# Two transformer blocks in one launch: how the second block's stages hand over to each other, and which engine copies and multiplies attention's probabilities

## The chip, the cores and the metric

One core of a Trainium2 chip runs the whole program. The metric is the device time of one launch in microseconds (us). Times are lower-is-better. The engines are TensorE (PE; PEld is its weight load), VectorE (DVE), ScalarE (ACT), GpSimd (POOL) and SyncE (SP), which issues most transfers.

## What is computed

The input is one sequence of 1024 tokens of width 1024, all in fp32. `first_block` has two layers: a projection, three token mixers (sliding-window attention, retention, gated linear attention), an output projection and a normed residual. `second_block`, which the change is about, has two layers of this form, cut to what matters:

```python
for l in range(DEPTH):                                   # DEPTH = 2
    hc = rmsnorm(h_ctx, g_pre_mix[l]) * (1.0 + csc1) + csh1      # 256 context rows
    hx = rmsnorm(x, g_pre_mix[l]) * (1.0 + sc1) + sh1            # 1024 rows
    q, k, v, u, gv, f = jnp.split(hx @ w_in[l], ...)             # and the same of hc (k, v alone in the last layer)
    attn = latent_window_attention(rope(q), rope(k), v, ck, cv, sink[l])   # band of 3 blocks of 128, plus 256 context keys, plus a sink
    sgu = spatial_gating(gelu(u), gelu(gv), w_sgu[l], b_sgu[l], g_sgu[l])
    four = fourier_mix(f)                                        # real part of a DFT over tokens and 64-wide groups
    y = merge_heads(attn, sgu, four, g_mix[l], w_out[l])         # three rmsnorms, then @ w_out
    x = x + g1 * rmsnorm(y, g_post_mix[l])
    hx2 = rmsnorm(x, g_pre_ff[l]) * (1.0 + sc2) + sh2
    x = x + g2 * rmsnorm(jnp.square(relu(hx2 @ w1)) @ w2, g_post_ff[l])    # D_FF = 4096; the same for h_ctx in layer 0
```

The softmax of attention is `exp(s - max) / (sum + exp(sink - max))`, and the probabilities that are multiplied by the values are already divided.

## The kernel before

**Products in three terms.** Activations lie transposed: a partition is one of 128 features, the columns are tokens, 512 at a time (two halves, b = 0 and 1) or the 256 of the context (b = NB). A weight matrix comes in chunks of 128 outputs x 1024 inputs, 512 KB each. To keep fp32 accuracy in the faster fp32r format, each operand is split into a rounded part and a rest. SyncE loads a chunk into `wraw` (L1690), ScalarE rounds it into `whi` (`split_high`, L1750), and GpSimd computes the rest `wlo` (`split_low`, L1736). The activations have `h_hi` (ScalarE, `high`, L1799) and `h_lo` (VectorE, `low`, L2120 on). TensorE then does 16 high products (h_hi and h_lo with whi, L2453) and 8 low products (h_hi with wlo, L2460) into one of two banks of `lin`. `wraw`, `whi`, `wlo` and the banks have two slots each, taken in turn by even and odd chunks. Semaphores count what is done: `w_hi`, `w_split`, `lin_done` (a chunk's last low product), `lin_free` (its bank evacuated). ScalarE's order of work in a chunk is: wait for `lin_done`, evacuate the bank, then round the weights of the chunk after next into the slot that this chunk has left. So `lin_done` also guards `whi`, and through it `wlo`.

**Stages of the second block.** Layer 0: projection of half 0 (`project`, 12 chunks), of the context, of half 1; the Fourier transform (`fourier`, 16 steps); the merges of half 0, half 1 and the context (`merge`, 8 chunks each); the feed-forwards of half 0, context, half 1 (`feed_forward`, 4 groups of 8 chunks of hidden units and 8 of outputs). Layer 1: the context's keys and values (2 chunks), both halves, the transform, two merges, two feed-forwards. Two of a projection's chunks are done token-major (`token_half`, L2562 on, products of L2574). Each engine has its own program, written out in the same order; they meet only through semaphores.

**Norms.** A norm's squares come from ScalarE (`square`, L1755) one feature block after another, VectorE adds them up (`add_square`, L2106), TensorE sums over partitions with a matrix of ones (L2430) and ScalarE makes the reciprocal root with a logarithm and an exponential (`root_pre`, `root_post`, `mix_roots`). VectorE scales the activations (`scale`, L2116), and `high` and `low` split them (L1804 or L1806; L2125 or L2127). The squares and scales of the next stage's norm are put beside a stage's chunks by hand; `high` and `low` of all 8 blocks come at the start of the next stage, after this stage's last chunk has read `h_hi` and `h_lo`. The first two chunks of a stage are multiplied as a pair (`high_pair`, L2464), each block as it becomes ready.

**Attention** is cut into steps of 4 heads and 128 queries, 40 in layer 0 and 32 in layer 1. Step i goes beside the i-th chunk or transform step, from the projection of half 1 on. TensorE's scores (L2533 to L2538); VectorE's maximum (`maximum`, L2148); ScalarE's exponentials (L1821); VectorE's reciprocal and its multiplication of the probabilities (`normalize`, L2175 and L2177); TensorE's transposes (`turn`, L2497), key and value head 0 and then 1, one chunk later; two copies out of `bankT` for each, by VectorE (L2166) and ScalarE (L1831); and the products with the values (L2559) at the head of the step after. On VectorE the additions of squares and the scales come before the copies (`attend`, L2180).

**The first block** uses the same chunks and slots in its own loop (L486 to L830, L1113 to L1163, L1395 to L1412).

## Time and profile before

| | |
|---|---|
| median of 3 runs | 4272.48 us (4271.44 to 4273.14) |
| the profiled execution | 4272.9 us, of which 4270.7 us from its first to its last instruction |
| mean granted TensorE clock | 0.956 of full speed |
| TensorE busy | 89% |
| VectorE, ScalarE, GpSimd busy | 51%, 40%, 36% |
| read from HBM | 397 MB, 95 GB/s over the span |

The first block ends at about 1313 us of the span, the second runs from there to the end. Busy shares are means over stages that differ. What counts is what TensorE waits for and where, and at which clock it runs afterwards. In the rows, a time in square brackets is how long the engine was idle just before the instruction, and behind the arrow stands what ended that idle time. Instructions of PE are grouped in a timeline only if they follow each other with the same operands.

### The profile page before, as it was taken

What the parts mean: (1) busy time and instruction counts of PE and PEld (TensorE: products, weight loads), DVE (VectorE), ACT (ScalarE), POOL (GpSimd) and SP (SyncE); (2) the same over time, 40 slices, a digit from 0 to 9 for tenths busy, and PEclk for the clock granted to TensorE, in tenths of its full rate; (3) what the DMA queues carried; (4) which work ended last, traced back from release to release, by engine and by line L of the source; (5) the groups of instructions that cost most, each with busy time, mean ns of one, the idle gap of its engine ahead of it and who ended that gap; (6) DMA issues with size and microseconds to landing.
All of it is one profiled execution on the core that took longest, in us unless ns stands there. A gap on an engine that the chain in (4) does not pass through costs nothing. (4 is left out here: it accounts for less than half of the span.)

```text
span 4270.7 us, 60415 instructions
## 1 busy us (share of the span) xinstructions
PE 3805.2 (89%) x22828; PEld 3059.4 (72%) x22828; DVE 2166.8 (51%) x2741; ACT 1714.6 (40%) x2935; POOL 1555.4 (36%) x704
## 2 busy tenths in 40 slices
PE   4989999999996798877999788999799779999997
PEld 3867767667665677656788777887677668877886
DVE  5435536445444566657325647325666664347225
ACT  3345345354353444444223334224444453234222
POOL 1433434334332322223444564443322224444443
PEclk8999999999998899988999999999899999999999
DMA  6423424333323221112232443332321122332223
GB/s 236 138 98 123 136 104 143 116 114 124 131 94 103 84 70 50 50 50 78 90 94 93 127 138 100 94 93 85 89 69 50 50 69 86 95 95 89 93 93 108
DMA packets 127195, 421.17 MB, mean 99 GB/s; under 512 B 17408, under 2 KB 19088, under 8 KB 126352
## 3 DMA queue, kind: packets, MB, share of 16 engines
q1 hardware_dynamic: 120080, 407.45, 29.6%
q10 hardware_dynamic: 6912, 10.90, 0.7%
q8 instruction: 141, 2.31, 0.2%
q14 instruction: 62, 0.51, 0.0%
HBM read 397.32 MB, written 6.29 MB: 95 GB/s over the span
## 5 line engine op out<-in xcount | busy, mean ns | idle before, releaser
L1739 POOL TENSOR_TENSOR wlo<-wraw,whi 128x1024 fp32r<-128x1024 f32 x454 | 1097.5, 2423 | 1859.4 <-ACT whi L1753 1858.9
L2453 PE MATMUL lin<-h_hi,whi 128*128 128x512 f32 (+1 forms) x2016 | 764.6, 386 | 107.1 <-DVE h_lo L2127 39.3
L2453 PE MATMUL lin<-h_lo,whi 128*128 128x512 f32 (+1 forms) x2016 | 749.0, 379 | 0.0
L1753 ACT ACTIVATE whi<-wraw 128x1024 fp32r<-128x1024 f32 x454 | 477.3, 1055 | 651.4 <-PE lin L2460 555.5
L2453 PEld LDWEIGHTS lin<-h_hi,whi 128*128 128x128 f32 x2016 | 398.0, 197 | 194.7 <-issue 112.5
L501 POOL TENSOR_TENSOR wlo<-wraw,whi 128x1024 fp32r<-128x1024 f32 x130 | 314.3, 2418 | 586.9 <-ACT whi L596 586.9
L2453 PE MATMUL lin<-a_hi,whi 128*128 128x512 f32 (+1 forms) x1280 | 479.4, 381 | 46.7 <-ACT whi L1753 38.8
L2453 PE MATMUL lin<-a_lo,whi 128*128 128x512 f32 (+1 forms) x1280 | 474.9, 377 | 0.0
L2460 PE MATMUL lin<-h_hi,wlo 128*128 128x512 f32 (+1 forms) x2016 | 461.5, 372 | 4.9 <-POOL wlo L1739 4.9
L2453 PEld LDWEIGHTS lin<-h_lo,whi 128*128 128x128 f32 x2016 | 397.5, 197 | 68.7 <-issue 3.3
L2460 PEld LDWEIGHTS lin<-h_hi,wlo 128*128 128x128 f32 x2016 | 352.0, 189 | 71.5 <-POOL wlo L1739 8.8
L2341 DVE TENSOR_TENSOR a_lo<-tmp,a_hi 128x512 fp32r<-128x512 f32 (+3 forms) x160 | 311.9, 1949 | 116.8 <-ACT a_hi L2025 114.3
L1122 PE MATMUL lin<-h_hi,whi 128*128 128x512 f32 x832 | 343.3, 413 | 8.2 <-DVE h_lo L846 8.2
L1122 PE MATMUL lin<-h_lo,whi 128*128 128x512 f32 x832 | 332.0, 399 | 0.0
L2453 PEld LDWEIGHTS lin<-a_hi,whi 128*128 128x128 f32 x1280 | 247.0, 193 | 104.1 <-issue 46.3
L2460 PE MATMUL lin<-a_hi,wlo 128*128 128x512 f32 (+1 forms) x1280 | 295.9, 375 | 2.4 <-POOL wlo L1739 2.2
L2453 PEld LDWEIGHTS lin<-a_lo,whi 128*128 128x128 f32 x1280 | 247.0, 193 | 46.6 <-issue 0.5
L2366 DVE TENSOR_TENSOR y<-lin,y 128x512 f32 (+3 forms) x120 | 76.5, 637 | 397.0 <-PE lin L2460 396.9
L2021 ACT ACTIVATE tmp<-lin 128x512 f32<-128x512 f32 (+1 forms) x160 | 88.4, 553 | 451.8 <-PE lin L2460 421.7
L2460 PEld LDWEIGHTS lin<-a_hi,wlo 128*128 128x128 f32 x1280 | 225.1, 188 | 52.5 <-POOL wlo L1739 4.6
L2106 DVE TENSOR_TENSOR tmp<-tmp 128x512 f32<-128x512 f32 (+1 forms) x165 | 166.3, 1008 | 176.9 <-ACT tmp L1763 172.1
L2338 DVE TENSOR_TENSOR tmp<-tmp 128x512 f32<-128x512 f32 (+1 forms) x160 | 132.1, 826 | 236.6 <-ACT tmp L2021 229.6
(339 smaller groups left out, 5998.7 us busy)
## 6 DMA issues: line engine op xcount, KB each, us to landing
wraw<-in_w SPq DMA_DIRECT2D x544, 512.0 KB, 3.5
mod_ring<-in_w_ada SPq DMA_DIRECT2D x96, 512.0 KB, 4.6
mod_ring<-in_w_mod SPq DMA_DIRECT2D x32, 512.0 KB, 4.6
wraw<-in_dft_tokens SPq DMA_DIRECT2D x32, 512.0 KB, 3.5
turn<-turn SPq DMA_DIRECT2D x144, 64.0 KB, 2.1
first_ring<-in_w_mod SPq DMA_DIRECT2D x16, 512.0 KB, 17.1
tmp<-tmp SPq DMA_DIRECT2D x80, 64.0 KB, 2.0
x<-in_x ACTq DMA_DIRECT2D x2, 2048.0 KB, 21.1
```

The costliest lines, as they stand in the source:

```text
L501: nc.gpsimd.tensor_tensor(wlo[:, s, :], wraw[:, s, :], whi[:, s, :].bitcast(F32), ALU.subtract)\
L1122: nc.tensor.matmul(bank[c % 2], whi[:, c % 2, k * P:(k + 1) * P], h[:, k, :], start=(k == 0 and h is h_hi), stop=False)
L1739: nc.gpsimd.tensor_tensor(wlo[:, s, 0:D], wraw[:, s, 0:D], whi[:, s, 0:D].bitcast(F32), ALU.subtract)\
L1753: nc.scalar.activation(whi[:, s, 0:D], wraw[:, s, 0:D], ACT.Copy).then_inc(*w_hi.one)
L2021: nc.scalar.activation(tmp[:, 4 + s, 0:w], bank[s][:, 0:w], ACT.Relu).then_inc(*lin_free.one)
L2106: nc.vector.tensor_tensor(total, total, tmp[:, slot, 0:w], ALU.add).then_inc(*sig["add"].one)
L2338: nc.vector.tensor_tensor(tmp[:, 2 + s, 0:w], tmp[:, 4 + s, 0:w], tmp[:, 4 + s, 0:w], ALU.mult).then_inc(*a_sq.one)
L2341: nc.vector.tensor_tensor(a_lo[:, unit, 0:w].rearrange("p o n -> p (o n)"), tmp[:, 2 + s, 0:w], a_hi[:, unit, 0:w].rearrange("p o n -> p ( ...
L2366: nc.vector.tensor_tensor(part, bank[s][:, 0:p.w], part, ALU.add).then_inc(*lin_free.one)
L2453: nc.tensor.matmul(bank[s][:, 0:p.w], whi[:, s, k * P:(k + 1) * P], h[:, k, 0:p.w], start=(k == 0 and h is parts[0]), stop=False)
L2460: last = nc.tensor.matmul(bank[s][:, 0:p.w], wlo[:, s, k * P:(k + 1) * P], parts[0][:, k, 0:p.w], start=False, stop=(k == KB - 1))
```

## The change

It has nine parts; the diff below is cut to the core of each.

1. *A semaphore for the high products.* `hi_used` counts chunks whose high products are done. `split_high` waits for it and no longer comes behind the evacuation: ScalarE rounds the weights of the chunk after next before it waits for `lin_done` (`refill`, and `split_high` at the head of `hidden` and in `outputs`). `split_low` gets a wait of its own for `lin_done`. The first block gets the same.

```diff
             def split_low(g, s):
                 pool.wait_ge(*w_hi.after(g, 1))
+                pool.wait_ge(*lin_done.after(g, -1))
...
             def split_high(g, s):
+                act.wait_ge(*hi_used.after(g, -1))
                 act.wait_ge(*chunk_in[s].after(g, 0))
...
             def hidden(gi, grp, j, s, w):
+                split_high(gi + 2, s)
                 act.wait_ge(*lin_done.after(gi, 1))
                 act.wait_ge(*a_ready.after(grp, j - 1))
                 nc.scalar.activation(tmp[:, 4 + s, 0:w], bank[s][:, 0:w], ACT.Relu).then_inc(*lin_free.one)
-                split_high(gi + 2, s)
```

2. *Chunks by blocks.* The last chunk of a projection, transform or merge, and the first of a projection or merge, are multiplied block by block, all three terms of a block together. After each block of a last chunk `h_used` is raised, and the next stage's `high` of that block waits for it. Both weight parts must be there before the first block.

```diff
+            def by_blocks(g, s, p, when=None, end=None):
+                pe.wait_ge(*lin_free.after(g, 1))
+                pe.wait_ge(*w_hi.after(g, 1))
+                pe.wait_ge(*w_split.after(g, 1))
+                for k in range(KB):
+                    if when:
+                        pe.wait_ge(*when(k))
+                    for n, (w, h) in enumerate(((whi, h_hi), (whi, h_lo), (wlo, h_hi))):
+                        last = nc.tensor.matmul(bank[s][:, 0:p.w], w[:, s, k * P:(k + 1) * P], h[:, k, 0:p.w],
+                                                start=(k == n == 0), stop=(k == KB - 1 and n == 2))
+                        if k == KB - 1 and n:
+                            last.then_inc(*(hi_used if n == 1 else lin_done).one)
+                    if end is not None and k < KB - 1:
+                        last.then_inc(*h_used.one)
...
-            def high(kind, n, k):
+            def high(kind, n, k, end=None, last=None):
                 act.wait_ge(*sig["scaled"].after(n.no, k + 1))
+                if end is not None:
+                    act.wait_ge(*(h_used.after(end, k + 1) if k < KB - 1 else lin_done.after(last, 1)))
```

3. *`high` and `low` of the next stage beside the last chunk.* On ScalarE, in the projection (the merge is alike, the transform does it in its last two steps); on VectorE all 8 `low` follow the last chunk's other work, in the merge ahead of the last square of the post-norm:

```diff
+                    if s == last:
+                        if nxt:
+                            for k in range(KB - 1):
+                                high("pre", nxt, k, end_of(l, "in", p.b), p.in_at + s)
+                        refill(p.in_at + s, s)
+                        if nxt:
+                            high("pre", nxt, KB - 1, end_of(l, "in", p.b), p.in_at + s)
...
             def merge(l, b):                      # VectorE
-                    if k == 0:
-                        for j in range(KB):
-                            low("mix", n, j)
...
+                    if k == KB - 1:
+                        for j in range(KB):
+                            low(kind, following, j)
                     add_square("post", post, k, POST_SUMS)
```

TensorE's sum for that post-norm stays at the head of the next merge.

4. *Norms earlier.* In the first projection the squares for the context rows come beside chunks 2 to 5 and those for half 1 beside chunks 5 to 8 (`sums_beside`, with two blocks of `y` as room for the latter); the context's projection makes none and scales half 1 at chunks 3 to 6. The merge's squares for the next merge come at chunks 1, 2 and 4 and its roots at 5 (before: 2 to 5, and 6); the transform's squares at steps 9 and 10 and its roots at 11 (before: 9 to 11, and 12), the scales at 12 to 14.

```diff
+        def sums_beside(l, b):
+            if b == 0:
+                return [(pre_mix(l, NB), 2, bankO), (pre_mix(l, 1), 5, bankT)] if l == 0 else [(pre_mix(l, 1), 5, bankO)]
+            return []
```

5. *Sums behind products.* TensorE's sum over partitions for a projection's norm and for the first feed-forward's norm comes after the chunk's high products instead of before them. In the feed-forward the sum for the last stage's post-norm comes after 4 chunks instead of 1, its root at chunk 3, and the updates of the residual come two a chunk at chunks 4 to 7 instead of one a chunk at 1 to 7.

6. *The probabilities' multiplication on ScalarE.*

```diff
+            def normalize(l, i):                  # ScalarE
+                r, n = i % 2, sum(blocks_of(step_of(l, i)[0])) * P
+                act.wait_ge(*rden_ready.after(STEP_AT[l] + i, 1))
+                for kv in range(2):
+                    nc.scalar.activation(probs[r][:, kv, 0:n], probs[r][:, kv, 0:n], ACT.Copy, scale=rden[:, r, kv:kv + 1])\
+                      .then_inc(*pn_ready.one)
...
-            def normalize(l, i):                  # VectorE
+            def denominators(l, i):
                 link(nc.vector.tensor_tensor(esum[:, r, :], esum[:, r, :], esink[:, r, :], ALU.add))
-                link(nc.vector.reciprocal(rden[:, r, :], esum[:, r, :]))
-                for kv in range(2):
-                    nc.vector.tensor_scalar(probs[r][:, kv, 0:n], probs[r][:, kv, 0:n], rden[:, r, kv:kv + 1], None, ALU.mult)\
-                      .then_inc(*pn_ready.one)
+                nc.vector.reciprocal(rden[:, r, :], esum[:, r, :]).then_inc(*rden_ready.one)
```

ScalarE's order in a step is: exponentials, the next weights (in the projection and the merge), the copy for head 0, the multiplications, then squares, weights (in the transform), evacuation, the copy for head 1.

7. *VectorE's copies first.* Its copy for head 0 and the reciprocal come before the additions of squares.

8. *Values turned into another bank.* The transposes of the values go to `bankO` instead of the chunk's own bank, so that bank is free once it is copied.

9. *The transform's last two steps by blocks* (`last_blocks`), with all three terms of a block together; the third sum of the mix norm goes to `bankO` where that is free.

## Rows read from the trace of the kernel before

**Rows 1.** Page, busy us of each engine, share of the span and instructions

```profile
PE 3805.2 (89%) x22828; PEld 3059.4 (72%) x22828; DVE 2166.8 (51%) x2741; ACT 1714.6 (40%) x2935; POOL 1555.4 (36%) x704
```

**Rows 2.** Busy by window: length, PE, PEld, DVE, ACT, POOL busy (count), clock, DMA, GB/s

```profile
1399.00:1463.00 64.00, 46.14 (x311) 42.79 (x310) 23.36 (x29) 33.20 (x54) 28.24 (x12) 0.84 0.32 99
1978.00:2350.00 372.00, 358.36 (x1542) 291.05 (x1542) 163.16 (x152) 120.89 (x168) 155.79 (x65) 0.99 0.29 92
```

**Rows 3.** Waits of TensorE by releaser: us in total, times, longest

```profile
PE lin L2453 <- ACT whi L1753: 71.2, 55, 5.8
...
PE lin L1144 <- ACT whi L596: 3.6, 4, 0.9
```

**Rows 4.** Timeline of TensorE at handovers: start, us, operation, [idle before]

```profile
1471.36 0.77 PE L2453 MATMUL lin<-h_hi,whi 128*128 128x512 f32 x1 [6.87 <-DVE h_lo L2127]
...
1765.90 0.76 PE L2453 MATMUL lin<-h_hi,whi 128*128 128x512 f32 x1 [3.00 <-DVE h_lo L2125]
...
3000.81 0.77 PE L2453 MATMUL lin<-h_hi,whi 128*128 128x512 f32 x1 [6.53 <-DVE h_lo L2127]
...
3016.60 2.54 PE L2574 MATMUL lin<-whi,h_hi 128*128 128x256 f32 x16 [2.44 <-ACT whi L1753]
...
3096.33 0.77 PE L2453 MATMUL lin<-h_hi,whi 128*128 128x512 f32 x1 [5.14 <-DVE h_lo L2127]
...
3450.17 1.10 PE L2430 MATMUL bankT<-tmp,ones 128*128 128x512 f32 x2 [2.65 <-DVE tmp L2106]
...
3519.83 0.73 PE L2453 MATMUL lin<-h_hi,whi 128*128 128x512 f32 x1 [5.19 <-DVE h_lo L2127]
```

**Rows 5.** Timeline of TensorE at sums over partitions of the next norm

```profile
1377.16 1.22 PE L2430 MATMUL bankO<-tmp,ones 128*128 128x256 f32 x2 [6.59 <-DVE tmp L2106]
...
1449.31 2.08 PE L2430 MATMUL bankO<-tmp,ones 128*128 128x512 f32 x2 [6.97 <-DVE tmp L2106]
...
3495.15 2.07 PE L2430 MATMUL bankT<-tmp,ones 128*128 128x512 f32 x2 [6.70 <-DVE tmp L2106]
```

**Rows 6.** Timeline of ScalarE and TensorE, from hidden units to outputs of a feed-forward

```profile
2032.69 0.60 ACT L2021 ACTIVATE tmp<-lin 128x512 f32<-128x512 f32 x1 [3.38 <-PE lin L2460]
2033.18 1.05 ACT L1753 ACTIVATE whi<-wraw 128x1024 fp32r<-128x1024 f32 x1
...
2124.49 0.47 PE L2453 MATMUL lin<-a_hi,whi 128*128 128x512 f32 x1 [1.37 <-ACT whi L1753]
```

**Rows 7.** Timeline of VectorE before the attending projection of layer 1

```profile
3086.01 9.51 DVE L2116 SCALAR_TENSOR_TENSOR staged<-x,cols,tmp 128x512 f32<-128x512 f32 x8
3095.44 5.38 DVE L2127 SCALAR_TENSOR_TENSOR h_lo<-staged,cols,h_hi 128x512 fp32r<-128x512 f32 x8
```

**Rows 8.** Timeline of GpSimd in the context's feed-forward

```profile
2419.26 4.75 POOL L1739 TENSOR_TENSOR wlo<-wraw,whi 128x1024 fp32r<-128x1024 f32 x2 [2.47 <-ACT whi L1753]
2426.49 4.95 POOL L1739 TENSOR_TENSOR wlo<-wraw,whi 128x1024 fp32r<-128x1024 f32 x2 [2.47 <-ACT whi L1753]
```

**Rows 9.** Attention: groups by form (busy, mean ns), then timeline rows of ScalarE and TensorE

```profile
L2177 DVE TENSOR_SCALAR staged<-staged,rden 128x640 f32<-128x640 f32 x128 | 72.4, 608 | 2.2
...
L1804 ACT ACTIVATE h_hi<-q 128x512 fp32r<-128x512 f32 x16 | 8.8, 626 | 1.7 <-DVE q L2116 1.7
...
1659.66 2.00 ACT L1753 ACTIVATE whi<-wraw 128x1024 fp32r<-128x1024 f32 x2 [0.90 <-PE lin L2677]
...
1693.79 1.30 PE L2497 MATMUL bankT<-ident,staged 128*128 128x128 f32 x5 [3.10 <-DVE staged L2166]
```

**Rows 10.** The chain that ended last, in order of time: start, us, line, count

```profile
3519.83 9.11 PE lin L2453 x32
3533.46 3.63 PE lin L2453 x16
3538.91 3.63 PE lin L2453 x16
...
3567.83 7.25 PE lin L2453 x30
```

More of the change, by code:

```diff
@@ L1677, in merge_point, with merge_squares, mix_bank, scales_at @@
             return MERGE_POINT + MERGE_ROWS[l].index(b) * KB + k
+        def merge_squares(k):
+            return {1: MIX_SQUARES[0:2], 2: MIX_SQUARES[2:4], 4: MIX_SQUARES[4:8]}.get(k, ())
+        def mix_bank(n, part):
+            if part < 2:
+                return turnT[part]
+            return turnT[0] if n.rows.l == 0 and n.rows.b == 1 else bankO
+        def scales_at(first, s):
+            return range(4 * (s - first - 5), 4 * (s - first - 4)) if 5 <= s - first < 7 else ()
         @block.sync
@@ L1902, in project @@
             def project(l, p):
-                n, nxt, attending = pre_mix(l, p.b), next_in(l, p.b), p.b == 1
-                if p.in_no and not (l and p.context):
-                    for k in range(KB):
-                        high("pre", n, k)
-                for s in range(2 if l and p.context else IN2):
+                nxt, attending, last = next_in(l, p.b), p.b == 1, 1 if l and p.context else IN2 - 1
+                for s in range(last + 1):
                     if l and p.b == 0 and s == 0:
@@ L1988, in merge @@
             def merge(l, b):
[L1989 removed]
+                p, post, g = Rows(l, b), post_mix(l, b), merge_at(l, b)
                 prev, nxt = before_merge(l, b), next_merge(l, b)
                 ff = pre_ff(l, FF_ROWS[l][0]) if nxt is None else None
[L1992 to L1993 removed]
+                kind, following = ("mix", nxt) if nxt else ("pre", ff)
                 if prev:
@@ L2599, in project @@
                 n, nxt, g, attending = pre_mix(l, p.b), next_in(l, p.b), p.in_at, p.b == 1
+                last = 1 if l and p.context else IN2 - 1
                 def ready(k):
                     return norms["pre"]["ready"].after(n.no, k + 1)
-                for s in range(2 if l and p.context else IN2):
+                for s in range(last + 1):
                     also = None
@@ L2626, in project @@
                         token_half(g + GV2, p, s - GV2, True)
-                    else:
+                    elif s and not ends:
                         low_products(g + s, s % 2, p, h_parts)
```

474 lines of the change are left out of this document (270 added, 204 removed).

## The prediction

> **What bounds the kernel now.** I read the page's busy line first. TensorE is busy for 3805.2 of 4270.7 us, no other engine for more than half [rows 1]. So the end is set by TensorE's work, its waits, and what a wait does to its clock. The busy time by stage shows where it waits: the projection of the 256 context columns keeps TensorE busy for 46.14 of 64 us at a granted clock of 0.84, while a feed-forward of 512 columns has 358.36 of 372 us at 0.99 [rows 2]. A granted clock of 0.84 is a mix of TensorE's two levels, 1.2 and 2.4 GHz, and in this trace the low level follows a wait. The list of waits says for whom: the largest sum, 71.2 us, is for ScalarE's rounded weights [rows 3]. The timeline of TensorE then shows four kinds of places.
>
> First, handovers, where a stage's last chunk is done and the next stage's activations still have to be rounded (ScalarE) and their rest taken (VectorE). Eleven of the eighteen stages begin after a handover that the diff touches; six such places stand in [rows 4]. Second, sums over partitions before which VectorE's additions are late [rows 5]. Third, the change from hidden units to outputs in the feed-forward [rows 6]. Fourth, attention's steps, with waits of a few us where the squares for the next norm are put between its copies [rows 9].
>
> Units: a chunk of 512 columns takes TensorE 5.45 us (two starts in the chain) at full clock, of which 3.63 us are its high products; the first pair of chunks takes 7.25 us for 30 matmuls in steady work and 9.11 us for 32 after a handover, 1.4 us more than 32 in proportion [rows 10]. So a wait of 5 us costs about 6.5.
>
> **The sum.** It is made against the profiled execution, 4272.9 us, which is 0.4 us above the median shown, 4272.48.
>
> (a) *Feed-forward, hidden to output.* The second chunk of the pair waits 1.37 us (the other 15 of these waits are as long or 0.12 us shorter), because ScalarE evacuates chunk 7 (0.60 us) and only then rounds the weights of chunk 9 (1.05 us) [rows 6]. The change puts the rounding in front, released by the high products, 1.8 us earlier. What is late next is the evacuation alone. 1.05 us less 0.1 us for the changed order gives 0.95 us, in four groups of each of four 512-column feed-forwards: 16 x 0.95 = 15.2 us gained. In the 256-column feed-forward nothing is gained. There GpSimd's splits come two by two every 7.23 us, 3.6 us a chunk [rows 8], paced by load, rounding, split and next load; new waits on finished chunks are met by then.
>
> (b) *Context projection of layer 0.* It loses the squares and the sum over partitions for the second half (6.97 us of wait, [rows 5]) to the first projection, and its handover in, so it should fall to the weights' pace: 12 x 3.6 = 43 us of the 64 in [rows 2], 1 us added for blocks that now want both weight halves first. 20 us gained.
>
> (c) *Into the attending projection of layer 0 and into layer 1's first half.* Waits 6.87 and 6.53 us [rows 4]. VectorE takes 5.38 us for eight rests [rows 7], 0.67 each, against TensorE's 5.45/8 = 0.68 us a block: once begun in the last chunk they keep pace. With 1.4 us of clock each and no more than 0.4 left over, 8 us gained each, 16.
>
> (d) *Into layer 1's second half.* Wait 5.14 us [rows 4]. Here the eight scalings end 9.51 us after they begin and the rests follow at once [rows 7]. That order stays, so rounding early helps little; the sum before it moves behind 3.63 us of products, and the gate with it. 4 us.
>
> (e) *Transform to first merge, twice.* Waits of 3.00 us [rows 4] plus the clock, 4.4 us each: 9 us.
>
> (f) *Merge to merge, three times.* Before, the post-norm's last square is added first and the sum over partitions follows (2.65 us of wait, [rows 4]). Now VectorE does the eight rests first, and that same sum still stands in front of the next merge's first products. 8 x 0.67 us, a split of GpSimd's to wait out (2.4 us) and the addition stand where the rests stood. 0 us for a 512-column merge, 1 for the 256-column one. This is the step where I expect less than the diff suggests.
>
> (g) *Merge to feed-forward.* In layer 1 the sum's wait of 6.70 us [rows 5] is overlapped by 3.63 us of products and the handover's 5.19 [rows 4] halves: 8 us. In layer 0 the last merge has 256 columns and VectorE's scalings of 512 columns bind it: 1 us.
>
> (h) *First projection.* It takes over the context rows' squares and their root on top of those of the second half. ScalarE's root now waits inside chunk 6, so the chain from raw query to transfer to rotation starts later; the sum after chunk 8 waits 6.59 us today [rows 5]. The 3.6 us of overlap and about 3 us for earlier weights are used up: 2 us lost, bounds 6.6 gained and 8 lost.
>
> (i) *Weights for the token-major chunks of layer 1.* A wait of 2.44 us [rows 4], for the rounding of two chunks' weights behind evacuations. 2 us gained.
>
> (j) *Attention, 72 steps.* VectorE gives up two multiplications of 0.61 us a step [rows 9]. ScalarE has no row for its version; it takes 0.63 us for a copy of 512 columns and 1.05 us for 1024 [rows 6, 9], so 640 columns lie between. I take 0.73 us, by the straight line through both. In odd transform steps ScalarE waits 0.90 us for TensorE before it rounds weights [rows 9], and 1.46 us are put in: 0.56 us late, passed on to the products with the values. Sixteen odd steps, half of them in quiet stretches: 5 us lost. In attending projections the step is longer, and the cover is the chunk itself. Where squares are made, VectorE's copies come first now, so the wait of 3.10 us [rows 9] goes; what is late next is ScalarE's last copy behind squares, weights and roots. Net 5 us gained there, and 3 in the first merge: 3 us in all. Bounds: 105 us lost (all 72 x 1.46) and 16 gained.
>
> (k) *Context feed-forward.* The updates of a 512-column residual move from one a chunk to two in the last four. VectorE has little room beside the splits: 4 us lost.
>
> (l) *First block.* Four waits of 0.9 us for weights [rows 3]: 2 us gained, bounds 4 gained and 8 lost, as its mixers' work on ScalarE now stands behind a rounding.
>
> 15.2 + 20 + 16 + 4 + 9 + 1 + 9 - 2 + 2 + 3 - 4 + 2 = 75.2 us: 4272.9 - 75.2 = 4197.7, so 4198.
>
> Two rules against the change. VectorE needs 0.61 us for a multiplication for which I allow ScalarE 0.73 [rows 9]. The Trainium skill, Perfetto Trace Analysis, section "Optimizing Scalar/DVE Operations", says that VectorE in a performance mode is the faster of the two, and that moving work off pays when it is saturated. By that rule (VectorE is busy for 51%) the move alone would gain nothing; the sum counts it as a loss of 5, so the trace agrees.
>
> Also, VectorE's addition beside a split takes as long as the split does: eight scalings take 9.51 us where eight rests take 5.38 [rows 7], the same element count. The Trainium skill, SBUF — State Buffer, section "SBUF: two separate sides", has it that GpSimd and an operation of VectorE with two inputs in SBUF exclude each other for a whole instruction; the trace agrees. What it would do here is rival C.
>
> **The rivals.**
> A, *ScalarE binds attention* (slower). The multiplications wait for VectorE's reciprocals, and in ScalarE's queue the weights, the copies and the evacuation stand behind them. If every step's 1.46 us reach TensorE, 105 us stand where (j) counted 5: 4198 + 100 = 4298. It decides once a step gives ScalarE over 0.90 us more than its wait. For it: that odd step. Against: only 40% busy [rows 1].
> B, *merges hand over fully too*. If the rests and the last addition end within the last chunk, the three merges save 8 us each and the late squares another 12: 4198 - 36 = 4162. For it: all scalings of four come a chunk earlier. Against: the order in (f).
> C, *GpSimd's splits now start as a chunk ends* and meet VectorE's evacuation there, instead of 1.7 us later. For 512 columns 2.4 us of delay is covered by a chunk. In the 256-column outputs it is not all covered; of the 2.4 us that each addition can wait I let a quarter through: 32 chunks x 0.6 us = 19, 4217.
> D, *VectorE paces every handover*. If the scalings end as late as in (d) everywhere, (c), (e) and half of (g) and (b) go: 16 + 9 + 4 + 10 = 39 us back, 4237.
>
> **How the numbers follow.** Forecast 0.46, B 0.18, D 0.16, C 0.10, A 0.10. About 0.2% (8.5 us) is what a measurement of this kernel can tell from no change. The forecast's own unknowns are (h), (j) and (l), some 20 us either way. The range runs from 4150, past B, to 4262, past D, and leaves out most of A. Faster takes all but A and a part of D with (h) at its worst: 0.87; within 0.2% 0.04; slower 0.09.
>
> **What would show it.** Right: no wait for rounded weights at the feed-forward pair over 0.5 us; a context projection near 43 us at a clock of 1; waits at the heads of the projections under 2 us; sums of the post-norm still waited for 7 us at the second merge; a transform about as long as before. Wrong: longer transform steps with waits for ScalarE's copies or multiplications (A), a merge that begins without a wait for the post sum (B), waits of over 1 us before each 256-column output chunk (C), rests that begin after the last chunk in most stages (D).

## The result, and the profile after

The changed kernel takes 4295.4 us (median of 5 runs, 4293.9 to 4297.2), the kernel before 4271.4 in the same session: a ratio of 1.0058, 95% interval 1.0044 to 1.0073. So it is slower by some 24 us, and 97 us above the forecast. The profiled execution has a span of 4295.4 us.

I read the busy line of the page first.

```profile
PE 3822.9 (89%) x22828; PEld 3074.9 (72%) x22828; DVE 2136.5 (50%) x2597; ACT 1852.1 (43%) x3079; POOL 1570.7 (37%) x704
```

TensorE is busy for 18 us more [rows 1], with the same number of instructions, at a mean granted clock of 0.953 for 0.956. It says nothing of where. That is in the stages, read off TensorE's timeline from the end of one stage's last product with weights to the end of the next one's, so that a handover's wait counts to the stage that it opens. Between the kernels below, a stage that the edit leaves alone differs by up to some 4 us; the effects of the multiplications and the rounding are larger.

| stage, us | before | after | the change |
|---|---|---|---|
| first projection | 86.0 | 102.0 | +16.0 |
| context projection, layer 0 | 63.6 | 48.0 | -15.6 |
| attending projections, two | 252.5 | 241.1 | -11.4 |
| transforms, two | 331.1 | 347.3 | +16.2 |
| merges, layer 0, three | 218.9 | 251.3 | +32.4 |
| merges, layer 1, two | 137.7 | 151.1 | +13.4 |
| feed-forwards of 512 columns, four | 1480.5 | 1461.7 | -18.8 |
| feed-forward of the context | 257.3 | 258.5 | +1.2 |
| context and first half, projections of layer 1 | 105.2 | 106.4 | +1.2 |

The rest is the first block, done 8 us earlier, and the end, 2 us shorter. Gains of some 56 us stand against losses of some 80, and three places hold nearly all of the losses: the merges (46 us), the transforms (16) and the first projection (16). The windows of four of these stages, in the kernel before and then in the changed one (boundaries; then busy time of TensorE, its weight loads, VectorE, ScalarE and GpSimd; granted clock, share and rate of the DMA engines):

```profile
1313.00:1399.00 86.00, 75.06 (x374) 62.70 (x374) 30.40 (x37) 30.21 (x44) 26.36 (x11) 0.91 0.41 132
...
1590.00:1759.00 169.00, 146.45 (x1166) 120.18 (x1164) 109.97 (x191) 73.66 (x169) 35.18 (x15) 0.96 0.16 48
1759.00:1851.00 92.00, 76.34 (x409) 55.71 (x409) 49.93 (x102) 44.33 (x103) 21.98 (x9) 0.93 0.17 52
1851.00:1926.00 75.00, 59.28 (x254) 45.32 (x252) 45.94 (x66) 35.20 (x69) 19.74 (x8) 0.86 0.16 49
```

```profile
1305.00:1407.00 102.00, 80.84 (x376) 66.32 (x377) 45.73 (x54) 41.85 (x63) 27.08 (x11) 0.87 0.36 115
...
1577.00:1755.00 178.00, 148.78 (x1171) 123.65 (x1170) 97.86 (x161) 102.07 (x209) 35.19 (x15) 0.94 0.15 45
1755.00:1868.00 113.00, 81.83 (x407) 60.71 (x405) 44.45 (x80) 50.16 (x115) 21.55 (x9) 0.86 0.14 42
1868.00:1956.00 88.00, 63.05 (x254) 48.27 (x254) 45.67 (x65) 40.31 (x83) 19.61 (x8) 0.83 0.15 47
```

In the first merge (third line of each) TensorE is idle for 31 us instead of 16, and its clock is 0.86 instead of 0.93. In the transform ScalarE's busy time goes from 74 to 102 us.

The waits of TensorE say for whom (us in total, times, longest):

```profile
PE bankO L2651 <- DVE staged L2243: 53.4, 16, 6.2
PE bankT L2503 <- DVE tmp L2181: 34.2, 8, 8.5
...
PE bankO L2651 <- ACT staged L1889: 24.0, 20, 3.2
...
PE lin L2527 <- ACT whi L1799: 6.4, 6, 1.5
```

The 71.2 us for rounded weights [rows 3] are down to 6.4, as meant. In their place stand attention's products with the values (into bankO), which wait for copies of the transposed probabilities by VectorE (L2243) and ScalarE (L1889).

**One merge step.** In the kernel before, VectorE, then GpSimd, then ScalarE, around the end of a chunk at 1794.05 (TensorE's last low product):

```profile
1795.80 0.68 DVE L2106 TENSOR_TENSOR tmp<-tmp 128x512 f32<-128x512 f32 x1
1796.52 0.56 DVE L2166 COPY staged<-bankT 128x384 f32<-128x384 f32 x1
...
1796.19 2.50 POOL L1739 TENSOR_TENSOR wlo<-wraw,whi 128x1024 fp32r<-128x1024 f32 x1 [7.89 <-ACT whi L1753]
...
1794.08 0.60 ACT L1763 ACTIVATE tmp<-lin 128x512 f32<-128x512 f32 x1 [0.43 <-PE lin L2460]
```

The step with the same squares in the changed kernel (now the merge's second chunk, before its third, by part 4), where the chunk ends at 1784.71, and then TensorE:

```profile
1786.38 2.04 DVE L2181 TENSOR_TENSOR tmp<-tmp 128x512 f32<-128x512 f32 x2 [2.66 <-ACT tmp L1809]
1788.46 0.56 DVE L2243 COPY staged<-bankT 128x384 f32<-128x384 f32 x1
...
1784.80 2.36 POOL L1784 TENSOR_TENSOR wlo<-wraw,whi 128x1024 fp32r<-128x1024 f32 x1 [10.74 <-PE lin L2536]
...
1783.76 1.55 ACT L1881 ACTIVATE staged<-staged,rden 128x640 f32<-128x640 f32 x2
1785.22 1.13 ACT L1809 ACTIVATE tmp<-u 128x512 f32<-128x512 f32 x2
1786.26 0.57 ACT L1809 ACTIVATE tmp<-lin 128x512 f32<-128x512 f32 x1
...
1789.16 0.29 PE L2651 MATMUL bankO<-staged,vx 128*64 128x128 f32 x1 [3.27 <-DVE staged L2243]
```

Two things have come together. ScalarE's multiplications (1.55 us) and the squares of the next norm stand in front of the post-norm's square, which begins 1.55 us after the chunk's end instead of 0.03. And GpSimd's split, whose rounded weights are ready long before, begins 0.09 us after the chunk's end instead of 2.14 and runs beside VectorE's additions. The second copy stands behind both: it begins 3.75 us after the chunk's end, where it began 2.47 us after it, and TensorE waits 3.27 us (0.74 us in the kernel before, at 1797.23).

**One transform step, odd.** ScalarE in the changed kernel, then TensorE:

```profile
1651.64 1.55 ACT L1881 ACTIVATE staged<-staged,rden 128x640 f32<-128x640 f32 x2 [0.15 <-DVE rden L2252]
1653.10 1.99 ACT L1799 ACTIVATE whi<-wraw 128x1024 fp32r<-128x1024 f32 x2
1654.99 0.36 ACT L1889 ACTIVATE staged<-bankT 128x256 f32<-128x256 f32 x1
...
1660.70 0.38 ACT L1889 ACTIVATE staged<-bankT 128x256 f32<-128x256 f32 x1
...
1655.40 0.32 PE L2651 MATMUL bankO<-staged,vx 128*64 128x128 f32 x1 [0.81 <-ACT staged L1889]
...
1661.17 0.74 PE L2589 MATMUL bankT<-ident,staged 128*128 128x128 f32 x5 [0.86 <-issue]
```

ScalarE's last copy of the odd step stands behind multiplications and two roundings, and TensorE waits 0.81 us for it. The even step has a wait of its own (0.86 us): the second head's transposes need `bankT` free, and begin 0.09 us after ScalarE's copy of the first head (1660.70 to 1661.08).

**The first projection**, VectorE, ScalarE, TensorE:

```profile
1367.63 0.69 DVE L2326 TENSOR_TENSOR q<-tmp 128x512 f32<-128x512 f32 x1
1368.36 1.67 DVE L2193 SCALAR_TENSOR_TENSOR staged<-xc,cols,tmp 128x256 f32<-128x256 f32 x4
1369.94 0.69 DVE L2181 TENSOR_TENSOR y<-y 128x512 f32<-128x512 f32 x1
...
1370.66 0.63 ACT L1809 ACTIVATE y<-x 128x512 f32<-128x512 f32 x1 [5.94 <-DVE y L2181]
1371.20 0.58 ACT L1938 ACTIVATE tmp<-lin 128x512 f32<-128x512 f32 x1
...
1371.87 0.80 PE L2527 MATMUL lin<-h_hi,whi 128*128 128x512 f32 x1 [5.91 <-ACTq L1940]
```

The second square of a pair waits for VectorE's addition of the first, which stands behind a rotation and four scalings; the evacuation of the query chunk (L1938) stands behind that square, and TensorE behind the evacuation. The next rotation needs that evacuation, so the delay goes round.

### The profile page after: what moved, and what is told of

It is laid out like the page before. It is cut to its first block and busy times, and to the rows that moved or that the text cites. A ratio compares the mean times of both kernels' runs of the same rounds, so it can differ in the third digit from the quotient of the medians.

```text
span 4295.4 us, 61401 instructions
## 1 busy us (share of the span) xinstructions
PE 3822.9 (89%) x22828; PEld 3074.9 (72%) x22828; DVE 2136.5 (50%) x2597; ACT 1852.1 (43%) x3079; POOL 1570.7 (37%) x704
## 5 line engine op out<-in xcount | busy, mean ns | idle before, releaser
L1799 ACT ACTIVATE whi<-wraw 128x1024 fp32r<-128x1024 f32 x454 | 476.3, 1056 | 1109.9 <-PE lin L2527 814.0
L2527 PE MATMUL lin<-h_hi,whi 128*128 128x512 f32 (+1 forms) x1856 | 701.8, 385 | 61.9 <-ACT y L2093 15.0
L2527 PE MATMUL lin<-h_lo,whi 128*128 128x512 f32 (+1 forms) x1856 | 688.1, 378 | 0.0
L2414 DVE TENSOR_TENSOR tmp<-tmp 128x512 f32<-128x512 f32 (+1 forms) x160 | 316.5, 1978 | 335.7 <-ACT tmp L2101 332.3
L2527 PEld LDWEIGHTS lin<-h_hi,whi 128*128 128x128 f32 x1856 | 363.6, 196 | 143.1 <-ACT y L2093 17.7
L2536 PE MATMUL lin<-h_hi,wlo 128*128 128x512 f32 (+1 forms) x1856 | 430.0, 375 | 2.5 <-POOL wlo L1784 0.9
L2527 PEld LDWEIGHTS lin<-h_lo,whi 128*128 128x128 f32 x1856 | 363.2, 196 | 61.8 <-issue 1.5
L2536 PEld LDWEIGHTS lin<-h_hi,wlo 128*128 128x128 f32 x1856 | 327.5, 190 | 66.3 <-POOL wlo L1784 6.0
L600 ACT ACTIVATE whi<-wraw 128x1024 fp32r<-128x1024 f32 x130 | 136.7, 1057 | 297.9 <-PE lin L1131 205.1
L2181 DVE TENSOR_TENSOR tmp<-tmp 128x512 f32<-128x512 f32 (+1 forms) x151 | 151.1, 1001 | 135.5 <-ACT tmp L1809 130.0
L1139 PE MATMUL lin<-h_hi,wlo 128*128 128x512 f32 x832 | 215.3, 401 | 0.0
```

Of the source, the lines that this page charges most:

```text
L600: nc.scalar.activation(whi[:, s, :], wraw[:, s, :], ACT.Copy).then_inc(*w_hi.one)
L1139: last = nc.tensor.matmul(bank[c % 2], wlo[:, c % 2, k * P:(k + 1) * P], h_hi[:, k, :], start=False, stop=(k == KB - 1))
L1799: nc.scalar.activation(whi[:, s, 0:D], wraw[:, s, 0:D], ACT.Copy).then_inc(*w_hi.one)
L2181: nc.vector.tensor_tensor(total, total, slot[:, 0:w], ALU.add).then_inc(*sig["add"].one)
L2414: nc.vector.tensor_tensor(tmp[:, 2 + s, 0:w], tmp[:, 4 + s, 0:w], tmp[:, 4 + s, 0:w], ALU.mult).then_inc(*a_sq.one)
L2527: last = nc.tensor.matmul(bank[s][:, 0:p.w], whi[:, s, k * P:(k + 1) * P], h[:, k, 0:p.w], start=(k == 0 and h is parts[0]), stop=False)
```

## The experiments

All ratios are to the kernel before, timed on the same chip; no kernel here leaves a part of the computation out. The first four change one thing each in the changed kernel.

**1. GpSimd's split held behind VectorE's addition.**

```
 for k in range(2, KB):            # the merges' chunks, unrolled
+    if k > 2:
+        pool.wait_ge(*norms["post"]["add"].after(post_mix(l, b).no, k - 2))
     split_low(g + k, k % 2)
```

> The changed kernel, but inside the merges GpSimd takes the split of a chunk's weights only when VectorE has added the square of the chunk before last. In the changed kernel the split starts as a chunk ends (1784.80) and the addition beside it takes 2.0 to 2.7 us for two where two took 1.4, and TensorE then waits 3.27 us for VectorE's second copy. Theory 1 (the collision of split and addition makes the merges slow): some 19 merge steps gain 1.3 to 2 us and a part of the clock, 25 to 45 us, so 4250 to 4270. Theory 2 (ScalarE's multiplications make the squares late): under 8 us. Theory 3 (a split held back comes too late for the chunk's low products): slower than 4295.

Measured: 4275.5 us, ratio 1.0015 (1.0005 to 1.0024), 20 us gained, just under theory 1's range and far over theory 2's. The three merges of layer 0 fall from 251.3 to 236.4 us. The pair of additions takes 1.42 us and the split begins when it is done:

```profile
1782.45 1.42 DVE L2193 TENSOR_TENSOR tmp<-tmp 128x512 f32<-128x512 f32 x2 [2.66 <-ACT tmp L1821]
...
1783.95 2.35 POOL L1784 TENSOR_TENSOR wlo<-wraw,whi 128x1024 fp32r<-128x1024 f32 x1 [13.82 <-DVE tmp L2193]
```

So the collision is real, at 0.6 us an addition pair here. What holding the split back costs by itself is not in this price: TensorE's longest wait for a chunk's rest (L2548) is now 4.3 us, where it was 0.3.

**2. Multiplications back on VectorE.**

```
-    for kv in range(2):       # ScalarE, normalize
-        nc.scalar.activation(probs..., probs..., ACT.Copy, scale=rden[:, r, kv:kv + 1]).then_inc(*pn_ready.one)
+    for kv in range(2):       # VectorE, behind the reciprocals
+        nc.vector.tensor_scalar(probs..., probs..., rden[:, r, kv:kv + 1], None, ALU.mult).then_inc(*pn_ready.one)
```

> The changed kernel with the multiplications by the reciprocals back on VectorE, in all 72 steps of a layer pair. Theory 1 (collision): the merges stay as long as they are to within 8 us, 4285 to 4300. Theory 2 (ScalarE's multiplications, 0.9 to 1.55 us a step, stand in front of the post-norm's square): some 19 merge steps and the last transform steps gain 1 to 1.5 us each and some clock, 20 to 35 us, so 4260 to 4275.

Measured: 4243.2 us, ratio 0.9936 (0.9919 to 0.9952). 52 us gained, more than any theory said, and not where theory 2 had it: 43 of the 52 come from the two transforms (177.6 to 155.7 us, 169.7 to 148.8), 8 from the merges of 512 columns. Windows of the transform and the first merge:

```profile
1576.00:1732.00 156.00, 141.93 (x1170) 117.79 (x1169) 106.70 (x198) 75.24 (x174) 35.47 (x15) 0.99 0.17 51
1732.00:1840.00 108.00, 80.06 (x406) 59.98 (x404) 53.91 (x95) 41.27 (x97) 23.02 (x9) 0.87 0.14 44
```

TensorE's idle time in the transform is halved (29 to 14 us), and its clock is 0.99 instead of 0.94.

**3. The merges' rounding back behind the evacuation.**

```
-    if k < KB - 1:
-        refill(g + k)
     turned(l, i - 1, 0)
     ...
     nc.scalar.activation(y[:, k, 0:p.w], bank[s][:, 0:p.w], ACT.Copy).then_inc(*lin_free.one)
+    if k < KB - 1:
+        refill(g + k)
```

> The changed kernel with ScalarE's rounding of the next weights in the merges back behind the evacuation of the chunk, as before (the last chunk of a merge excepted). GpSimd's splits then begin 2 us after a chunk's end. Theory 1: as much as in the run that holds the split behind the addition, 25 to 45 us, 4250 to 4270, with additions of 0.69 us. Theory 2: ScalarE still has the multiplications in front of the square, but a rounding (1.05 us) less; a third of the excess at most, 4280 or above.

Measured: 4256.6 us, ratio 0.9968 (0.9956 to 0.9981). 39 us gained: theory 1's range. The first merge takes 96.0 us instead of 112.8, and a pair of additions 1.42 us there (1791.65). But it is twice what holding the split back gave, so the early rounding may have a second price; experiment 11 looks for it.

**4. VectorE's second copy first.**

```
-    add_square("post", post, k, POST_SUMS)
     turned(l, i - 1, 1)
+    add_square("post", post, k, POST_SUMS)
```

> The changed kernel with VectorE's second copy of a merge step ahead of its addition of the post-norm's square, nothing else moved. Theories 1 and 2 both say that the addition is late and the copy stands behind it: the waits of 3.27 us for the copy go in 19 steps, 40 to 60 us with the clock, 4235 to 4255. If instead the copy is late by itself (the transposes), nothing: 4290 to 4298. If the sums of the post-norm take over as the wait, half: about 4270.

Measured: 4274.5 us, ratio 1.0013 (1.0003 to 1.0022). 21 us gained, near the third expectation. From the first merge to the last of layer 0, TensorE's waits for VectorE's copies fall from 28.5 to 12.0 us, and those for ScalarE's copies rise from 2.7 to 10.8. The sums of the post-norm, which that expectation named, are waited for as before (9.7 us for 9.8).

The next two take single parts of the change into the kernel before.

**5. In the kernel before, copies first.**

```
+    attend(l, i)                      # VectorE, transform and merges
     (additions and scalings of the next norm)
-    attend(l, i)
```

> The kernel before with one part of the change alone: in the transform and the merges VectorE takes its first copy and the reciprocals with the multiplications ahead of the additions and scalings. The changed kernel with the multiplications back on VectorE has transforms of 155.4 and 148.5 us where the kernel before has 172.9 and 166.0. Theory A (the copies' place gives the transforms those 17.5 us each): 30 to 45 us gained, 4228 to 4242. Theory B (the earlier rounding of weights gives them): under 12 us gained, 4260 or above.

Measured: 4245.7 us, ratio 0.9946 (0.993 to 0.9963). 22 us gained, between the two. The 17.5 us of the expectation set unlike stretches against each other: its 172.9 and 166.0 us run on into the merge's first scores and products with the values, 3.9 us each. By one boundary the transforms take 169.0 and 162.1 us in the kernel before, 159.9 and 151.7 here, and 155.7 and 148.8 in experiment 2. The first of them, here:

```profile
1583.00:1743.00 160.00, 143.22 (x1169) 118.98 (x1168) 107.04 (x192) 73.31 (x168) 35.29 (x15) 0.98 0.16 50
```

So 9 and 10 us of the 13 each come with the place of the copies, as theory A has it. The other 4 and 3 come with what the changed kernel has besides; which part of it was not tried alone.

**6. The same, with the multiplications on ScalarE.**

```
     turned(l, i - 1, 0)
+    act.wait_ge(*rden_ready.after(STEP_AT[l] + i, 1))
+    for kv in range(2):
+        nc.scalar.activation(probs..., probs..., ACT.Copy, scale=rden[:, i % 2, kv:kv + 1]).then_inc(*pn_ready.one)
```

> The same, with the multiplications by the reciprocals moved to ScalarE too, where the change has them. Theory 2 (a ScalarE multiplication of 640 columns stands in the chain from exponentials to transposes to copies in every transform step): 35 to 50 us slower than the run with the copies alone. Theory 2' (it costs only where ScalarE also rounds early, as in the changed kernel): within 10 us of it.

Measured: 4287.5 us, ratio 1.0042 (1.0027 to 1.0056). 42 us above the run with the copies alone, as theory 2 has it: this part is worth a loss of 42 to 52 us on either side of the change. Of it some 18 us fall in the transforms, 9 in the first merges of the two layers and 9 in the attending projections. Another 4 are no effect of the edit: in the profiled execution the first block, which is the same in both, ends that much later.

The rest are built on the changed kernel with experiments 2 and 3 put together.

**7. Experiments 2 and 3 together.**

> The changed kernel with both single gains put together: the multiplications on VectorE (measured alone: 52 us) and the merges' rounding behind the evacuation (alone: 39 us). The first acts in the transforms and the second in the merges, so if they lie on different waits they add: about 4204, faster than the kernel before by 65 us. If the multiplications on VectorE give back in the merges what the rounding gained (VectorE has the copies and the additions there): 4220 to 4235.

Measured: 4200.9 us, ratio 0.9837 (0.982 to 0.9853). 52 and 39 make 91, and 94 are gained: the two lie on different waits. With both taken back, layer 0's merges are at 220.3 us, where the kernel before has 218.9 and the changed one 251.3, and layer 1's at 133.7, where it has 137.7 and 151.1. So the two account for the merges' whole loss; what the other parts do there one by one was not tried. The waits for rounded weights that they bring back sum to 23.8 us (6.4 in the changed kernel). Windows of the transform and of two merges:

```profile
1576.00:1731.00 155.00, 140.88 (x1162) 117.29 (x1161) 105.78 (x195) 74.40 (x172) 35.51 (x15) 0.99 0.18 52
1731.00:1823.00 92.00, 76.34 (x410) 56.92 (x409) 53.12 (x96) 42.00 (x98) 22.21 (x9) 0.91 0.17 52
1823.00:1901.00 78.00, 60.45 (x258) 46.15 (x257) 45.71 (x72) 37.24 (x76) 19.43 (x8) 0.87 0.15 48
```

**8. Transposes inside the last chunk, copies ahead.** TensorE's transposes of a merge's last chunk go into its blocks (the first before block 0, the second after block 1), and both engines' copies go ahead of roundings and rests; VectorE's second copy is ahead of the addition in all steps.

```
     elif k == KB - 1:
+        turn(l, i - 1, 0)
+        by_blocks(g + k, k % 2, p, None, end_of(l, "merge", b), lambda: turn(l, i - 1, 1))
```

It was made because of what the trace of experiment 3 shows where the first merge of layer 0 hands over to the second, ScalarE and then TensorE:

```profile
1848.16 2.17 ACT L1852 ACTIVATE h_hi<-q 128x512 fp32r<-128x512 f32 x4
...
1846.34 0.38 PE L2589 MATMUL bankT<-ident,staged 128*128 128x128 f32 x2
...
1856.92 0.48 PE L2651 MATMUL bankO<-staged,vc 128*64 128x128 f32 x2 [8.68 <-issue]
```

The blocks are done when the transpose begins (1846.34), and ScalarE rounds only after it. At this handover the pieces don't overlap at all.

> The last kernel with the transposes of a merge's last chunk put inside its products by blocks, and both engines' copies ahead of the roundings and rests handed over, and VectorE's second copy ahead of its addition in all merge steps. In the trace of the late rounding ScalarE begins to round the next activations only at 1848.16, after the last block (1846.34), since it waits for the transpose behind the blocks, and TensorE then waits 8.68 us for a copy behind the rests. Theory: the handover between merges of layer 0 gains 6 to 9 us, the steps 0.5 to 1 us each, 15 to 25 us in all with the clock against the run without it: 4180 to 4190. Rival: the sum of the post-norm, whose addition now comes after the rests, takes the wait over: within 5 us of it.

Measured: 4200.0 us, ratio 0.9837 (0.9821 to 0.9854), as without it: the rival. The second merge of layer 0 falls from 77.9 to 72.0 us, the first rises from 92.0 to 97.9.

**9. The second half's squares back in the context projection.** Its sum and its scalings move with them, the scalings to chunks 6 to 9.

```
-    return [(pre_mix(l, NB), 2, bankO), (pre_mix(l, 1), 5, bankT)] if l == 0 else ...
+    return [(pre_mix(l, NB), 2, bankO)] if l == 0 else ...       # b == 0
+    return [(pre_mix(l, 1), 1, bankO)] if l == 0 and b == NB else []
```

> The kernel with the multiplications on VectorE and the late rounding in the merges, and in layer 0 the squares, the sum and the scalings of the second half's norm moved from the first projection back to the context projection, where the kernel before has them, though earlier in it (squares from its second chunk). Theory (these squares are what makes the first projection 102.1 us where it was 86.0): it falls back to 86 to 90 us, the context projection rises from 48.3 us to 50 to 54, 8 to 12 us gained, 4189 to 4193. Rival (the first projection is long by ScalarE's rounding order, not by the squares): it stays above 98 us, and the time at 4201 to 4208.

Measured: 4197.8 us, ratio 0.9831 (0.9815 to 0.9848), 3 us below experiment 7 and between the two expectations. The first projection falls from 102.1 to 88.3 us, as the theory has it, so the squares are what makes it long. But the context projection rises from 48.3 to 56.5, more than the 54 allowed, at a granted clock of 0.91 (1.00 in the changed kernel).

**10. Evacuation ahead of the squares.** In the first projection ScalarE evacuates the chunk first, and VectorE takes the second half's additions ahead of its scalings.

```
+    early = p.in_no == 0 and s in (3, 4, 5, 7, 8)
+    if early:
+        chunk_end(p, s)
     for n, first, ps in sums_beside(l, p.b):
         (squares)
-    chunk_end(p, s)
+    if not early:
+        chunk_end(p, s)
```

> The kernel with the multiplications on VectorE and the late rounding in the merges, and in the first projection ScalarE's evacuation ahead of the squares and VectorE's additions for the second half ahead of its scalings of the context. In the changed kernel the evacuation stands behind a square that waits 5.94 us for an addition behind a rotation and four scalings, and TensorE waits 5.91 us for it. Theory (the ping-pong of squares and additions holds up the evacuation): 5 to 10 us gained, 4191 to 4196. Rival (the sum after chunk 8 takes the wait over, as additions still wait for rotations): 4198 to 4204.

Measured: 4188.2 us, ratio 0.9809 (0.9793 to 0.9826), 13 us below experiment 7 (12 by the two ratios, as they were timed on different chips), more than the 5 to 10 expected. The first projection takes 92.5 us, and the context projection stays short:

```profile
1305.00:1398.00 93.00, 77.89 (x379) 63.81 (x380) 46.73 (x55) 42.20 (x64) 26.74 (x11) 0.91 0.39 127
1398.00:1447.00 49.00, 39.32 (x305) 36.88 (x303) 18.74 (x20) 25.07 (x40) 29.03 (x12) 0.98 0.40 120
```

The wait for the evacuation falls from 5.91 to 2.84 us; the sum after chunk 8 takes some of it over, 7.21 us where it was 4.75. This is the fastest of the kernels: 2% below the kernel before.

**11. Multiplications on VectorE, split behind the addition, rounding early.** The edits of 1 and 2.

> The changed kernel with the multiplications on VectorE (4243 alone), rounding as early as the change has it, and only GpSimd's split in the merges held behind VectorE's addition. Theory (the whole 42 us that the late rounding gains beside it is the collision of split and addition): 4201 to 4210. Rival (a part is ScalarE's rounding itself, ahead of square and copy, as when the split alone was held back with the multiplications on ScalarE, 20 of 39 us): 4220 to 4226.

Measured: 4216.3 us, ratio 0.9875 (0.9858 to 0.9891). 27 of the 42 us that the late rounding gains beside VectorE's multiplications come back with the split alone. It lies between the two expectations. So the split's early start is worth at least some two thirds. The other third is open: it goes with the early rounding in another way, with the split of the third chunk, which this edit leaves free, or with the price of holding a split back. TensorE's longest wait for a chunk's rest is 4.6 us here (L2548), and 0.3 for the same products in experiment 7.

**12. The gains together.** Experiment 10, and 8 for a merge's last chunk alone.

> The changed kernel with all that single runs gained: the multiplications on VectorE, the merges' rounding behind the evacuation, the first projection's evacuation ahead of its squares, and, in a merge's last chunk alone, the transposes inside the products by blocks and both engines' copies ahead of the roundings and rests. With the transposes inside the blocks and VectorE's second copy first in every step, the first merge of layer 0 had gone from 92.3 to 98.1 us and the second from 77.9 to 72.0. Theory (the loss was the addition, put behind the copy where it meets GpSimd's split; the gain was the handover): 92 and 72 us, 5 to 7 us below 4188, so 4181 to 4183. Rival (the handover only moves the wait from the second merge to the first): 4186 to 4190.

Measured: 4190.7 us, ratio 0.9814 (0.9801 to 0.9828), the rival. The second merge keeps its gain (71.7 us), the first takes 96.3 instead of 92.0. The wait moves:

```profile
1811.10 0.41 PE L2599 MATMUL bankT<-ident,staged 128*128 128x128 f32 x2 [3.73 <-DVE staged L2244]
...
1822.00 2.05 PE L2511 MATMUL bankT<-tmp,ones 128*128 128x512 f32 x2 [3.55 <-DVE tmp L2182]
```

A wait of 7.72 us for the values' products has become one of 3.73 us for a copy, inside the last chunk of the first merge, and one of 3.55 us for the sum of the post-norm.

## Why the prediction was wrong

It said 4198 us and faster, with 0.87; the changed kernel is slower, at 4295.4. With the multiplications on VectorE and the merges rounding late the same kernel takes 4200.9. That nearness is in part luck: (h) missed by 14 us and (e) by all of its 9, while the copies first give the transforms 19.5 us (experiment 5), where (j) forecast 8 us of gains for all of attention. But it says what the sum lacked above all: two prices, 52 and 39 us.

**(j) is the step that failed first.** I took ScalarE's multiplication of 640 columns to last 0.73 us, by a straight line; its group has 0.82 us (VectorE's 0.61, [rows 9]):

```profile
L1881 ACT ACTIVATE staged<-staged,rden 128x640 f32<-128x640 f32 x128 | 99.0, 821 | 19.5 <-DVE rden L2252 18.2
```

The exponentials of the same 640 columns take 790 ns in the kernel before (L1821); that row was nearer than a line through two copies. That is the small part. The large one is where it lies. I charged 0.56 us to eight odd transform steps a kernel, because ScalarE waits 0.90 us there. But odd and even steps are one ring: scores, exponentials, reciprocals, multiplication, transposes, copies, values' products, and TensorE goes round it in every step. The copies of step i stand behind the multiplications of step i+1 in ScalarE's queue, and in the steps with squares TensorE waited already (3.10 us, [rows 9]). Measured, a transform loses 21 to 22 us in the changed kernel, 1.3 us a step, and the whole 42 to 52 us. The bound of 105 held it; the value taken was nearly the other end, chosen by one row of one kind of step. Rival A named the mechanism, with 0.10 and a price of 100 us: the mechanism was right, at half that price, and it deserved the larger chance. Its test, ScalarE busy for only 40% of the span, was the wrong one: in the transform it is 57% after (102.07 of 178 us), and what counts is the order in its queue.

**(f) held where it looked, and not beside it.** It has the post-norm's sum late behind the eight rests, and at the head of layer 1's second merge that sum is waited for 8.46 us, where it was 2.65 [rows 4], so the 0 us were still too kind:

```profile
3497.95 2.04 PE L2503 MATMUL bankT<-tmp,ones 128*128 128x512 f32 x2 [8.46 <-DVE tmp L2181]
```

But the steps between the handovers are what became longer. No term of the sum holds them: I had moved the roundings earlier and counted this as free, and it cost 39 us (experiment 3), and rival C saw GpSimd's split at the end of a chunk meet VectorE, but put it in the context's outputs (19 us). There it costs nothing that can be seen: that feed-forward has 258.5 us for 257.3. It costs in the merges, where VectorE's addition and then its copy stand in the chain to TensorE, and the evidence for the order there was in the trace of before. Rival C had the right mechanism in the wrong stage. The group of the feed-forward's multiplications, before and after, shows the meeting without a price; there the next chunk seems to hide it, as these stages got shorter:

```profile
L2338 DVE TENSOR_TENSOR tmp<-tmp 128x512 f32<-128x512 f32 x128 | 92.8, 725 | 213.3 <-ACT tmp L2021 212.6
```

```profile
L2414 DVE TENSOR_TENSOR tmp<-tmp 128x512 f32<-128x512 f32 x128 | 269.8, 2108 | 297.7 <-ACT tmp L2101 296.8
```

**(h) was mis-sized:** 2 us lost forecast, 16 measured, twice the bound of 8. I had the longer chain from raw query to rotation, but not that the additions and scalings of a second norm stand in front of the square that stands in front of the evacuation. Experiment 10 gave 10 of it back by order alone.

**(e) failed:** 4.4 us gained at each first merge forecast, but the wait at the head is 4.90 us after (3.00 before, [rows 4]), since the first thing in TensorE's queue is now the values' products, whose copy stands behind the rests:

```profile
1762.08 0.30 PE L2651 MATMUL bankO<-staged,vx 128*64 128x128 f32 x1 [4.90 <-issue]
```

**(c), (d), (i): half.** Into the attending projection of layer 0 the wait of 6.87 us [rows 4] is 0.35, as forecast, and the stage is 8.4 us shorter than before once the multiplications are back on VectorE (experiment 2), for the 8 of (c).

```profile
1461.71 0.50 PE L2555 MATMUL lin<-h_hi,whi 128*128 128x512 f32 x1 [0.35 <-DVE h_lo L2204]
```

Into layer 1's second half 5.14 is 0.17, better than the 4 us of (d). But the 6.53 us into its first half are 1.17 and 1.73 us between blocks, and the context's two chunks ahead of it now have waits of 3.96 and 0.84 us (2.42 us in three waits before), so nothing was gained, and the two stages together lose 1.2 us. The wait of 2.44 us of (i) is 1.22.

**(a) held:** the four waits of 1.3 to 1.4 us in the first feed-forward are 0.3 us each, 1.05 us for 0.95. The last feed-forward, with no handover in it that the change touches, is 3.9 us shorter, for 3.8 forecast. **(b)** gave 15.6 of 20: 48.0 us at a granted clock of 1, for the 44 forecast. **(g)** held: the last merge of layer 1 and the head of the feed-forward give 5.5 and 2.1 us, for 8. **(k)** lost 1.2 us, for 4. **(l)** stays open: the second block begins 7.9 us earlier than before, but with an unchanged first block it began 6.5 us (experiment 5) and 2.3 us (experiment 6) earlier too.

Rival B, a full handover in the merges, didn't come: the waits of 8.46 and 4.90 us above. Rival D, rests that pace every handover, came in one place: into layer 1's context chunks and first half TensorE waits for `h_lo` between blocks. In (c) and (d) it didn't, by the waits of 0.35 and 0.17 us.

Of the two rules that spoke against the change one would have warned me. The Trainium skill, Perfetto Trace Analysis, section "Optimizing Scalar/DVE Operations", has moving work off VectorE pay when VectorE is saturated. It was busy for 51% [rows 1], and the move lost 42 to 52 us: the runs agree. I had let that rule stand for a loss of 5, and wrote that the trace agreed when only my own sum did. The exclusion that the Trainium skill, SBUF — State Buffer, section "SBUF: two separate sides", tells of agrees with experiment 1, where additions of two inputs from SBUF take 1.42 us a pair without a split and 2.04 beside one. The pair is not longer by a whole split: the split had 0.78 us to go when it began.

## What to carry to other kernels

An operation moved to an idle engine is priced by what stands behind it in that engine's queue, in the tightest kind of step, and not by the engine's busy share; if it lies on a ring that is gone round 72 times, 0.4 us more of engine time a step (two instructions of 0.21 us more) can be 0.6 to 0.7 on the path. A wait taken away starts the next engine earlier, so look up in each stage what that engine will then run beside: here a split that starts 2 us earlier showed no price in the feed-forwards and cost 20 to 27 us in the merges (39 to 42 with the rounding that released it). And a handover by pieces overlapped here only where no instruction that ends behind the pieces (a transpose, a sum) stood in front of their consumers in any queue; the order of the three queues around it can be written down before anything is run.

## What was not expected of the hardware

Two losses of different kinds were additive to within 4 us (52 and 39 against 94), although each also lowered TensorE's clock. In the transform an idle time of 29 instead of 14 us cost 22 us: the clock granted was 0.94 instead of 0.99, so half as much again as the waits themselves. And ScalarE's multiplication by a column of scales takes 0.82 us for 640 columns and 0.50 for 256, so 0.84 ns a column and 0.28 us besides, within 0.03 us of its exponential of the same shape in the same trace (0.79 us).
